# Who issues the expert weights: down weights from ACT's DMA queue, gate and up weights from the sync engine's

## What is computed

```python
def hierarchical_moe(xn, wg, bg, we, be, w_gate, w_up, w_down):
    ...                                   # top-1 of 4 groups, top-2 of its 8 experts: 32 experts
    xs = xf[tok]                          # tokens sorted by expert
    h = jax.nn.silu(lax.ragged_dot(xs, w_gate, sizes)) * lax.ragged_dot(xs, w_up, sizes)
    y = lax.ragged_dot(h, w_down, sizes) * weights.reshape(-1)[order][:, None]
    out = jax.ops.segment_sum(y, tok, num_segments=T)
```

## Time and profile before

| | us |
|---|---|
| median of 3 runs (2117.55 to 2118.31) | 2118.07 |
| the profiled execution | 2118.72 |
| its span in the trace | 2116.9 |
| PE busy, share of the span | 1953.1, 92% |
| ACT busy, share of the span | 525.6, 25% |
| DMA queue of SP, share of 16 engines over the span | 57.6% |

### The profile page before, as it was taken

The page is one execution under the profiler, slowest core; times in us unless marked ns, Lnnn a source line. Parts: engine busy times, 40 slices in busy tenths (PEclk is TensorE's granted clock), DMA queues, the critical chain, the costliest instruction groups (busy, mean ns, idle before and its releaser), DMA issues.

```text
span 2116.9 us, 22950 instructions
## 1 busy us (share of the span) xinstructions
PE 1953.1 (92%) x9528; PEld 1244.7 (59%) x9528; DVE 785.4 (37%) x1201; ACT 525.6 (25%) x941; POOL 115.1 (5%) x131
## 2 busy tenths in 40 slices
PE   7997899987899999999799979989888999999997
PEld 5875577756544444444388869977565444444443
DVE  3355545535232222222433254364343222222322
ACT  3246333423101110110234332334321111111010
POOL 3100000001000000000100031000010000000000
PEclk9998899998899999999999989999888999999999
DMA  6210133212599999999732312232023999999996
GB/s 222 99 60 1 60 111 119 80 35 97 211 417 409 410 406 412 410 411 411 308 106 87 133 39 80 100 130 100 22 80 155 417 412 404 415 408 411 407 411 273
DMA packets 100138, 491.13 MB, mean 232 GB/s; under 512 B 7720, under 2 KB 15960, under 8 KB 50752
## 3 DMA queue, kind: packets, MB, share of 16 engines
q1 hardware_dynamic: 96928, 478.18, 57.6%
q0 software_dynamic: 2512, 9.33, 1.3%
q10 hardware_dynamic: 592, 2.11, 0.3%
HBM read 487.47 MB, written 2.10 MB: 231 GB/s over the span
## 4 chain that ended last, share of the span: by engine, by line
PE 85%; DVE 8%; ACT 3%; issue 2%; POOL 1%; DMA 0%; ACTq 0%; DVEq 0%; POOLq 0%
PE ps L580 24%; PE ps L800 21%; PE ps L815 11%; PE ps L770 6%; PE ps L792 6%; PE ps L577 5%; PE ps L755 2%; PE ps L748 1%; PE ps L593 1%; PE ps L686 1%; PE ps L610 1%; DVE wl L467 1%; PE ps L632 1%; PE ps L784 1%; PE ps L681 1%
## 5 line engine op out<-in xcount | busy, mean ns | idle before, releaser
L800 PE MATMUL ps<-ring,xg 128*64 128x512 f32 x1536 | 346.3, 596 | 0.0
L467 DVE TENSOR_TENSOR wl<-ring,wh 128x512 fp32r<-128x512 f32 x280 | 192.0, 695 | 409.2 <-ACT wh L458 408.3
L458 ACT ACTIVATE wh<-ring 128x512 fp32r<-128x512 f32 x280 | 174.8, 630 | 446.6 <-PE ps L580 361.0
L1766 DVE TENSOR_TENSOR x<-ps,x 128x1024 f32<-128x1024 f32 x128 | 150.7, 1220 | 335.3 <-PE ps L792 335.3
L580 PE MATMUL ps<-wh,ah 128*128 128x512 f32 x544 | 216.4, 398 | 13.6 <-DVE al L1473 6.2
L800 PEld LDWEIGHTS ps<-ring,xg 128*64 128x64 f32 x1536 | 104.8, 137 | 198.4 <-issue 194.5
L580 PE MATMUL ps<-wl,ah 128*128 128x512 f32 x544 | 215.0, 395 | 0.0
L580 PE MATMUL ps<-wh,al 128*128 128x512 f32 x544 | 214.3, 394 | 0.0
L815 PE MATMUL ps<-ring,hT 128*64 128x512 f32 x768 | 171.9, 596 | 1.4 <-ACT hT L1253 1.4
L770 PE MATMUL ps<-oh,xnh 128*128 128x256 f32 x512 | 132.7, 297 | 5.2 <-DVE oh L1784 5.2
L770 PEld LDWEIGHTS ps<-oh,xnh 128*128 128x128 f32 x512 | 98.4, 192 | 52.5 <-issue 52.5
(11 more groups left out here) (252 smaller groups left out, 2618.4 us busy)
## 6 DMA issues: line engine op xcount, KB each, us to landing
ring<-in_moe_w_gate SPq DMA_DIRECT2D x96, 1024.0 KB, 9.4
ring<-in_moe_w_up SPq DMA_DIRECT2D x96, 1024.0 KB, 8.2
ring<-in_moe_w_down SPq DMA_DIRECT2D x96, 1024.0 KB, 8.7
slot<-in_moe_w_up SPq DMA_DIRECT2D x32, 1024.0 KB, 9.2
slot<-in_moe_w_gate SPq DMA_DIRECT2D x32, 1024.0 KB, 9.5
slot<-in_moe_w_down SPq DMA_DIRECT2D x32, 1024.0 KB, 8.8
ring<-in_x_wkv SPq DMA_DIRECT2D x16, 1024.0 KB, 5.2
ring<-in_c_w_in SPq DMA_DIRECT2D x16, 1024.0 KB, 5.2
```

What stands on the lines that cost most here:

```text
L458: act.activation(wh[:, t % STAGE, :], ring[:, unit % RING, 512 * s:512 * (s + 1)], ACT.Copy).then_inc(wh_ready, 1)
L467: dve.tensor_tensor(wl[:, t % STAGE, :], ring[:, unit % RING, 512 * s:512 * (s + 1)], wh[:, t % STAGE, :].bitcast(F32), ALU.subtract).then ...
L800: mm = pe.matmul(ps[p * SLOTS:(p + 1) * SLOTS, bank, :], xg[:, b % 2, k, r * P + p * SLOTS:r * P + (p + 1) * SLOTS], w(p)[:, k % 4, :], st ...
L1766: return dve.tensor_tensor(x[:, m, :], ps[:, bank:bank + 2, :].rearrange("p a n -> p (a n)"), x[:, m, :], ALU.add)
```

## The change

SP's loop now issues only units 0 to 7 of a pair (gate and up). The four down units, D0 and D1, are issued by ACT, on ACT's own DMA queue, behind ACT's existing wait for the end of G1 and ahead of its silu.

```diff
--- before.py
+++ after.py
@@ -522,7 +522,7 @@
                 for q in range(PAIRS):
-                    for j in range(2 * STAGES):
+                    for j in range(8):
                         u = u0 + 2 * STAGES * q + j
                         free_slot(u, l)
                         src, cols = expert_unit(l, q, j)
@@ -1278,6 +1278,10 @@
                     act.wait_ge(stage_used, STAGES * (q0 + q) + 2)
+                    for j in range(8, 2 * STAGES):
+                        u = PLAN["moe", l][0] + 2 * STAGES * q + j
+                        src, cols = expert_unit(l, q, j)
+                        act.dma_start(slot(u, cols), src).then_inc(ring_full[SLOT[u]], 16)
                     after(act, S["h_ready"], q0 + q)
                     silu().then_inc(S["silu_done"], 1)
```

## The result

The changed kernel takes 2218.82 us (median of 4 runs, 2210.15 to 2221.72) against 2118.19 us before (the three runs of the table and a fourth): a ratio of 1.047, 95% interval 1.043 to 1.050. It is 100 us slower. The forecast was 2299.5 us, range 2200 to 2360: the direction and the place were right, the size was 1.8 times too large.

What follows compares the result with a forecast made beforehand. PE was taken to set the pace, with the DMA engines nearly full (0.7 us per pair to spare). 31 x (4.15 us late D1 + 1.7 us clock) = 181 us on 2118.72 gave 2299.5 us for the median, range 2200 to 2360.

Steps and rivals of the forecast that it cites:

- The bound and the place: In the expert stretches PE sets the pace, DMA engines have 0.7 us per pair to spare; PE would wait at D1.
- That alone costs nothing: D0 issued 5.62 us later, at the end of G1: no cost if D0 and D1 have the DMA engines to themselves.
- D0 and D1 no longer stand ahead of G0' and G1': SP's and ACT's queues share the DMA engines at half rate; D1 lands 4.15 us late in each counted pair.
- the fixed part: Time between a DMA's issue and landing beyond its transfer: taken as 3.4 us, bounds 2.6 and 4.2.
- PE's pause costs clock: After each wait for D1, about 3.4 us at half speed lose 1.7 us; bounds 0 and 3.4 us.
- The count of pairs: 31 of the 32 pairs would be late, all but the last of layer 1.
- ACT issues four DMAs ahead of its silu: The silu moves from 712.06 to about 713.6; its reader starts at 721.12, so cost 0, with 7 us of cover.
- The lateness: How late D1 lands after PE needs it at 15.81: 4.15 us a pair, bounds 3.35 to 4.95.
- the forecast case: Queues share and one short low-clock stretch follows each pause: 2275 to 2324, from 2248 if half falls in the pause; 50%.
- the rival without clock loss: Queues share, D1 is late, but no clock is lost: 2222 to 2271, middle 2247; chance 17%.
- The rival of an unequal share: ACT's queue gets more than half; at a share of 0.6 D1 is 1.96 us late, 2179 in all; chance 9%.

Runs made afterwards that it cites:

- the run with one queue: Kernel before, all twelve units on SP's queue, but SP issues D0 only at the end of G1: 2122.27 us, ratio 1.0025.
- the filler: Changed kernel with two extra matmuls (FILL = 2) on PE between D0 and D1, read by nobody: 2211.81 us, ratio 1.0465.
- e4_silu_first: Changed kernel with ACT's silu put ahead of its four DMA issues: 2220.80 us, ratio 1.0491.
- e11_hold_1us: Changed kernel, but SP holds G0' 1.0 us longer, until the first half of the mix behind U0 has ended: 2181.75 us, ratio 1.0329.
- e10_hold_2us: Changed kernel, but SP holds G0' 2.0 us longer, until both halves of the mix behind U0 have ended: 2160.39 us, ratio 1.0228.

## Why the prediction was right, and too large

**The bound and the place: right.** PE set the pace and the DMA engines had 0.7 us per pair to spare. The wait came at D1 and not at D0, in every pair but one of those that I had counted, and nothing else was late.

**"That alone costs nothing" (the later issue of D0): nearly.** 5 us, by the run with one queue.

**"D0 and D1 no longer stand ahead of G0' and G1'": right, mis-sized.** Two terms of this sum were off, both in the same direction. I took 3.4 us for the fixed part, the middle of 2.6 and 4.2. A first unit shows 2.4, which lies outside both bounds: the 4.2 was read in the middle of a stream, and this burst starts on idle engines. And I took 3.44 us as the time that ACT's queue has to itself, issue to issue. From the landing of the last unit, 731.17 + 17.6, it follows as 22.4 − 17.6 = 4.8 us, if the fixed part is 2.4; by bytes it is 2.18 / 4.19 of 10 us, 5.2. The queue that joins later gets its first bytes later after its issue, 3.3 us against 1.0. Why isn't shown; that its packets stand behind what the engines already hold is a guess. 4.15 − 1.0 − 1.3 gives 1.8, the pause of this pair.

On average over the 30 pairs it is 2.39 us, because some are longer, and the trace says which. Its queue q8 (the kind "instruction") now and then carries one packet of 16 KB. In 13 of the 30 pairs such a packet falls between 4 and 17 us after ACT's first issue, while the two queues share. In these pairs the last D1 unit lands 18.2 to 19.5 us after the first issue, in the other 17 pairs 17.3 to 18.0 us. The pauses of the 13 sum to 39.3 us (3.0 each), those of the 17 to 32.4 (1.9 each, with 3.9 in the first pair of layer 1, where PE comes to D1 earlier). One of the 13 is the pair at 763.95, with a pause of 2.96 us; in 763:783 the view of the queues has:

```profile
q8 instruction: 1, 0.02, 0.3%
```

In the pair at 731.17 there is no such packet. 0.3% of 16 engines over 20 us is 1 us of one engine, about what these pairs are late. That the packet is the cause fits in size and place, but no run here tests it.

**"PE's pause costs clock": right, mis-sized.** 32.3 / 30 = 1.1 us per pair, not 1.7. The pauses are shorter than the 4 us that I had worked with, and only 12 of the 30 go with a stretch at 0.50. That the pauses do it, and not the queues, is shown by the filler: same queues, clock back.

**The count of pairs.** 30, not 31. The last pair of layer 0 has SP's loads beside it, as I said, but they have rows of 2 KB, and ACT's packets of 8 KB then get most of the bytes (this stretch, 1076:1080 us of the changed kernel):

```profile
q10 hardware_dynamic: 176, 1.28, 75.8%
q1 hardware_dynamic: 186, 0.38, 24.5%
```

**"ACT issues four DMAs ahead of its silu": right**, at nothing; the issues took 2.1 us and not 1.5.

With 30 x (2.39 + 1.08) = 104 in place of 31 x (4.15 + 1.7) = 181, the sum closes.

**The range was luck in part.** The lateness of 2.39 us lies outside its own bounds, 3.35 to 4.95, and the 2219 us lie below all that the forecast case allowed (2248 to 2324) and below the rival without clock loss (2222 to 2271). The measured time is inside 2200 to 2360 only because the lower end was drawn past those cases. The rival of an unequal share had a lateness of 1.96 us, near the usual pause of 1.8, but by a mechanism that isn't there: the shares are equal (52.1% and 48.3%), and it was the late start of SP's bytes that helped ACT's queue.

The Trainium skill's rule on queues ("DMA: Bandwidth & Descriptors", sections "Queues, rings and completion order" and "Issuing engines are not separate DMA queues") is turns by packet, and no gain but issuing time from a second issuing engine. The traces agree as far as they go: 85 packets against 83 for rows of different size, and no gain in any run. What it doesn't speak of is the loss: an order of importance that one queue gave for free was given up.

## What to carry to other kernels

When the DMA engines are nearly full, the order in which one queue sends is a schedule by urgency. Splitting it over two queues doesn't add rate; it takes rate from the transfer that is needed first and gives it to one that is needed later. If a second issuer is wanted, let its transfers start a transfer's length ahead of the competing ones (D0 at the end of G0 made the same split cost nothing), or give the urgent queue the longer rows (16 of the 100 us were left). And price a PE stall in dense matmuls at more than its length. Here it was 45% more, and in the three other kernels with such pauses and no filler, by PE's busy time over that of before, 33% (`e4_silu_first`, 24.7 on 74.2 us), 29% (`e11_hold_1us`, 13.7 on 47.2) and 37% (`e10_hold_2us`, 10.8 on 29.3).

## What the runs showed of the hardware

- Two queues with work take turns packet by packet: with rows of equal size 52.1% and 48.3% of the time; with 8 KB against 2 KB rows 85 and 83 packets, 0.67 and 0.17 MB in 2 us.
- A queue that joins while another is being sent gets its first bytes out later: SP's first packets begin 3.3 us or more after their issue at 734.60 (in 737.9:738.1), ACT's on idle engines 1.0 us after theirs at 731.17 (in 732.1:732.3).
- In the pairs where one 16 KB packet of the instruction queue q8 falls into the time in which the two queues share, the last D1 unit lands at 18.2 to 19.5 us, in the others at 17.3 to 18.0.
- A DMA issued by ACT behind an activation goes out when the activation starts (728.87 against 728.86), not when it ends.
- Of 30 PE pauses of 1.4 to 4.7 us in dense matmuls, 12 go with 3.4 us or more at 1.2 GHz, none of them one of the 13 pauses under 1.9 us; with 63.5 / 32 = 2.0 us of matmuls put into each, the stretch 600:1020 is at a granted clock of 1.00.
